# Forty-seven one-pass products appended after the last tile of a two-block transformer kernel

## The reference, cut to what matters

```
merged = jnp.sum(gates * br, axis=2)
x = x + jnp.einsum('bsd,de->bse', merged, w_out[l])
```

## Time and profile before

| | us |
|---|---|
| median of 3 runs | 974.19 |
| lowest and highest run | 973.27, 974.43 |
| span of the profiled execution, first to last instruction | 970.7 |
| median less that span | 3.5 |
| TensorE busy in the span | 960.0 |
| TensorE weight loads busy | 858.6 |
| VectorE busy | 610.2 |
| ScalarE busy | 485.9 |
| GpSimd busy | 216.9 |

### The profile page before, as it was taken

One profiled execution on the slowest core, in us unless ns is written; L12 is line 12 of the kernel. 1 busy time (PEld: TensorE's weight loads), 2 busy tenths in 40 slices (PEclk: granted clock), 3 DMA queues, 4 the chain that ended last, 5 costly groups with the idle time before them and its releaser, 6 DMA issues.

```text
span 970.7 us, 17117 instructions
## 1 busy us (share of the span) xinstructions
PE 960.0 (99%) x7053; PEld 858.6 (88%) x7053; DVE 610.2 (63%) x827; ACT 485.9 (50%) x729; POOL 216.9 (22%) x177
## 2 busy tenths in 40 slices
PE   9999999999999998999999999999999999999998
PEld 8989999999889896899999997778787878999996
DVE  5867554554589899764445447747574646856664
ACT  6446434434364475743443446456545555647452
POOL 0005980000023330000000000414662704920100
PEclk9999999999999999999999999999999999999999
DMA  8764855656554522365565573555455635562461
GB/s 274 221 224 149 275 176 180 196 186 195 190 180 159 175 88 75 126 231 176 186 202 174 186 239 116 198 172 175 142 172 172 190 108 174 176 210 94 136 213 43
DMA packets 119635, 168.73 MB, mean 174 GB/s; under 512 B 5556, under 2 KB 88596, under 8 KB 119572
## 3 DMA queue, kind: packets, MB, share of 16 engines
q1 hardware_dynamic: 119140, 167.66, 53.3%
q10 hardware_dynamic: 432, 0.19, 0.1%
HBM read 165.38 MB, written 2.46 MB: 173 GB/s over the span
## 4 chain that ended last, share of the span: by engine, by line
PE 92%; DVE 4%; ACT 1%; POOL 1%; DMA 1%; issue 1%; SPq 0%; ACTq 0%; DVEq 0%
PE ps L465 26%; PE ps L467 25%; PE ps L466 25%; PE ps L919 2%; PE ps L906 2%; PE ps L892 2%; DVE wlo_sb L445 1%; POOL b_inv_sb L2455 1%; PE ps L553 1%; DMA raw_sb<-w_in_even 1%; PE ps L492 1%; PE ps L566 1%; PE ps L726 1%; PE ps L2077 1%; PE ps L563 1%; PE ps L558 1%
## 5 line engine op out<-in xcount | busy, mean ns | idle before, releaser
L445 DVE TENSOR_TENSOR wlo_sb<-raw_sb,whi_sb 128x2048 fp32r<-128x2048 f32 x143 | 332.7, 2328 | 201.1 <-ACT whi_sb L422 201.1
L422 ACT ACTIVATE whi_sb<-raw_sb 128x2048 fp32r<-128x2048 f32 x143 | 273.9, 1916 | 180.6 <-PE ps L467 163.3
L465 PE MATMUL ps<-hhi_sb,whi_sb 128*128 128x256 f32 x992 | 278.4, 281 | 0.9 <-DVE wlo_sb L445 0.5
L466 PE MATMUL ps<-hlo_sb,whi_sb 128*128 128x256 f32 x992 | 276.9, 279 | 0.0
L467 PE MATMUL ps<-hhi_sb,wlo_sb 128*128 128x256 f32 x992 | 276.8, 279 | 0.0
L465 PEld LDWEIGHTS ps<-hhi_sb,whi_sb 128*128 128x128 f32 x992 | 186.5, 188 | 3.0 <-issue 1.2
L466 PEld LDWEIGHTS ps<-hlo_sb,whi_sb 128*128 128x128 f32 x992 | 186.5, 188 | 0.9
L467 PEld LDWEIGHTS ps<-hhi_sb,wlo_sb 128*128 128x128 f32 x992 | 186.4, 188 | 0.0
L465 PE MATMUL ps<-whi_sb,hhi_sb 128*128 128x512 f32 (+2 forms) x304 | 119.6, 394 | 0.3 <-DVE qkl_sb L2341 0.2
L467 PE MATMUL ps<-whi_sb,hlo_sb 128*128 128x512 f32 (+2 forms) x304 | 116.8, 384 | 0.0
L466 PE MATMUL ps<-wlo_sb,hhi_sb 128*128 128x512 f32 (+2 forms) x304 | 116.7, 384 | 0.0
(11 more groups left out here) (335 smaller groups left out, 1345.8 us busy)
## 6 DMA issues: line engine op xcount, KB each, us to landing
raw_sb<-w_in SPq DMA_DIRECT2D x45, 1024.0 KB, 5.2
raw_sb<-ffn_gate SPq DMA_DIRECT2D x22, 1024.0 KB, 5.3
raw_sb<-ffn_up SPq DMA_DIRECT2D x22, 1024.0 KB, 5.3
raw_sb<-ffn_down SPq DMA_DIRECT2D x22, 1024.0 KB, 5.0
raw_sb<-w_in_even SPq DMA_DIRECT2D x8, 1024.0 KB, 8.4
raw_sb<-w_in_odd SPq DMA_DIRECT2D x8, 1024.0 KB, 5.1
raw_sb<-w_branch SPq DMA_DIRECT2D x6, 1024.0 KB, 5.1
scratch_sb<-bias_rows_dram SPq DMA_DIRECT2D x40, 128.0 KB, 3.0
```

The source lines that it names most:

```text
L422: nc.scalar.activation(place(whi, n0), in_raw(n0), ACT.Copy).then_inc(hi_ready, 1)
L445: nc.vector.tensor_tensor(place(wlo, n0), in_raw(n0), place(whi, n0).bitcast(F32), ALU.subtract).then_inc(lo_ready, 1)
L465: nc.tensor.matmul(dst, l_hi, r_hi, start=first, stop=False)
L466: nc.tensor.matmul(dst, l_hi, r_lo, start=False, stop=False)
```

## The change

Behind the four tiles of the last projection TensorE makes 47 more one-pass products. They read the last weight tile, `w = place(whi, N_OUT2 + 3)`, and 128 columns of `hhi`, both of which are complete by then, and write PSUM bank 6 (in the last eight banks 6 and 7 in turn), which nobody reads afterwards. In front of them stand three waits on the last uses of banks 5 to 7.

```diff
+            w = place(whi, N_OUT2 + 3)
+            s = hhi[:, 6, 0:P]
+            pe.wait_ge(*RELEASED[-1])
+            pe.wait_ge(*RELEASED[-2])
+            pe.wait_ge(*RELEASED[-3])
+            columns = (
+                w[:, 0:256], w[:, 8:264], w[:, 2:258],
+                w[:, 0:512].rearrange("p (a b) -> p a b", b=2)[:, :, 0],
+                w[:, 0:256].rearrange("p (a b) -> p b a", b=2),
+                w[:, 0:256].rearrange("p (a b) -> p b a", a=2),
+                w[:, 0:512].rearrange("p (a b) -> p a b", b=16)[:, ::2, :],
+                w[:, 0:512].rearrange("p (a b) -> p a b", b=8)[:, ::2, :],
+                w[:, 0:256].rearrange("p (a b c) -> p b a c", a=2, c=8),
+                w[:, 0:2048].rearrange("p (a b) -> p b a", a=16)[:, 0:16, :],
+                bc(w[:, 0:16], 16, 1))
+            for v in columns:
+                for _ in range(3):
+                    nc.tensor.matmul(ps[:, 6, 0:256], s, v, start=True, stop=True)
+            for v, l, d in ((w[0:64, 0:256], hhi[0:64, 6, 0:P], ps[:, 6, 0:256]),
+                            (w[:, 0:256], hhi[:, 6, 0:32], ps[0:32, 6, 0:256])):
+                for _ in range(3):
+                    nc.tensor.matmul(d, l, v, start=True, stop=True)
+            for k in range(4):
+                nc.tensor.matmul(ps[:, 6 + k % 2, 0:256], s, w[:, 0:256], start=True, stop=True)
+            for k in range(4):
+                nc.tensor.matmul(ps[:, 6 + k % 2, 0:512], s, w[:, k * 512:k * 512 + 512], start=True, stop=True)
```

## The result

| | before | changed |
|---|---|---|
| median of 4 runs, us | 974.31 | 977.79 |
| span of the profiled execution, us | 970.7 | 976.0 |
| time of that execution, us | not recorded | 977.82 |

The ratio is 1.0041 with a 95% interval from 1.0029 to 1.0053: slower by more than the 0.2% that the prediction set as its line, as forecast, and inside the range. The single number, 978.7, was 0.9 us too high, though the span came out 0.8 us longer than predicted (976.0 against 975.2). These two don't fit together by themselves; experiments 1 and 4 take them up.

A forecast was written before the change was run, and what follows sets the result against it. TensorE, busy 960.0 of 970.7 us, was taken as the bound, with 2.9 us of cover at the end. Appended 5.02 + 0.93 + 0.27 + 1.19 = 7.41 us lengthen the span by 4.52: 974.19 + 4.52 = 978.7 us, range 977.2 to 981.0.

The forecast's parts named there:

- The cover of 2.9 us: Between TensorE's last product and SyncE's drain, appended TensorE work costs nothing for 2.9 us; every us beyond lengthens the span.
- The three waits and the start: Before the added products: waits already met, 0 us (other bound 0.15); first added product starts 0.233 us behind the last one.
- Contiguous products: Added products start 0.117 us apart at 256 columns (43, 5.02 us) and 0.233 at 512 (four, 0.93 us).
- Steps: Twelve added products whose moving operand has a step: 0.216 us each instead of 0.117, 1.19 us more in all.
- the pair: TensorE's moving operand is read two elements at a time; non-adjacent ones are read as two, 0.10 us more a product.
- signs of being wrong: In the profile after: forms 4 and 5 differing from 6 and 10, or any stepped product above 0.25 us, among others.
- The second rival: Only far steps (forms 6 and 10) fall to 0.216 us, forms 4 and 5 don't: +3.9 us, 978.1; chance 0.22.
- Shape changes: Among the added products, three changes of shape, back to full included, cost 0.09 us each, 0.27 us in all.
- Overlap: Added products run two at a time and the cover swallows them: 974.3 to 976.0 us, not slower; chance 0.04.
- The clock: TensorE goes on without a pause at the end, so all 47 added products run at the 2.4 GHz level.
- The sum: 7.41 us of TensorE behind 967.54, plus 0.26 for drain and barrier: span 975.21 against 970.69, 4.52 us more.
- The base: The 3.5 us outside the span stay, so the 4.52 us are added to the median of before, 974.19 us.

The follow-up runs named there:

- experiments 1 and 4: 1: the kernel before run again without edit, 973.40 us against 973.65. 4: the changed kernel run again with more runs, 978.62 us against 973.40 for before.
- Experiment 6: Changed kernel with its 47 products replaced by thirteen moving-operand views, four times each behind four contiguous products; one run, 0.11 to 0.285 us a product.

## Why the prediction was right, point by point

- **The place.** "The cover of 2.9 us" hides what is appended, and what exceeds it is paid in full: shown by 24, 35 and 51 products (0.1, 1.1 and 3.4 us), and by the same 47 costing 7.4 us where there is no cover.
- **The three waits and the start** cost nothing: the first added product starts 0.24 us behind the last real one.
- **Contiguous products** at 0.117 and 0.233 us: as measured, forms 1 to 3, 7 to 9, 11, 14 and 15.
- **Steps.** The step of the argument that failed is the pair: "a pair that isn't adjacent must be read as two". The total survived by luck, because errors of both signs cancel. Twelve products at 0.10 us extra made 1.19 us. Measured: forms 4 and 5 have 6 x (0.231 - 0.117) = 0.68 (forecast 0.59), form 6 nothing (0.30), form 10 3 x (0.27 - 0.117) = 0.46 (0.30): 1.14 us together. Experiment 6 puts four columns a line in the place of the pair, and a surcharge at distances of 256 and 512 bytes for form 10. Two of the prediction's own signs of being wrong came true with that: forms 4 and 5 differ from 6 and 10, and form 10 takes more than 0.25 us.
- **The second rival** (only far steps cost) fails on form 4, which costs 0.23, and on form 6, which costs nothing. Its page, the Trainium skill's "SBUF — State Buffer", section "Specifications (TRN2)", is borne out in that lines are 16 bytes: runs of 4 cost 0.12 us from a boundary and 0.23 from 4 or 8 bytes behind it. Its two hits a line are not enough for TensorE's one-pass products; step 2 has two and costs 0.23. The measurement decides.
- **Shape changes.** The term "3 x 0.09 = 0.27" measured 0.10 + 0.11 into 64 rows and 0.09 + 0.02 on to 128 rows with 32 columns, 0.32 us in all, and nothing for the third: a size slightly off and a rule that was wrong. The earlier trace rows could not tell rows from columns.
- **Overlap** (the case on the other side) didn't happen: no two added products start less than 0.11 us apart. They are 0.117 us apart at 256 columns and 0.23 at 512. The trace disagrees with the 131 ns at 512 columns of the Trainium skill's "TensorE: Matmul & The Clock Gate", section "Back-to-back issue gap", after the change as before.
- **The clock.** The forecast took the 2.4 GHz level for all 47: the granted clock is 1.00 over 967.5 to 976 us.
- **The sum.** 7.41 us of TensorE were forecast; from 968.08 to the last product's start (975.74 less its 0.39) and one more distance of 0.23 are 7.50. The span grew by 4.52 in the forecast and by 4.6 in the trace, and the time by 4.6 at full clock.
- **The base.** "The 3.5 us outside the span stay" was wrong: in all but one of the executions of before that list both it is 1.75 to 1.93 us. Taking 1.8 us for the profiled execution too, the other 1.7 us were the distance from its short span to the median of others; its own time isn't on record. It didn't touch the forecast difference. That 978.7 lies 0.9 us above the measured 977.79 comes from its base: 974.19, the median of before, is 1.1 us above the 973.13 that before has at full clock, and three of the four executions of the changed kernel are at full clock.

## What to carry to other kernels

Work appended to an engine cost nothing here as long as that engine ended before the last store had landed, and what lay beyond was paid in full; find that moment by putting the engine's drain beside the queue that waits for the output. For one-pass fp32 products lay the moving operand out so that each 16-byte line gives four columns close together: 256 columns then took 0.12 us. Views that gave fewer took 0.22 to 0.235 us, and steps of 256 or 512 bytes up to 0.285. Compare a profiled span with its own execution's time, not with a median of others, and compare executions that list the same clock.

## What was not expected of the hardware

- Two places read in turn are slightly faster than contiguous columns: 0.11 against 0.117 us.
- Elements needn't be distinct or in order: each 4th element four times over costs 0.12 us, as if it were contiguous.
- Going between 64 and 128 rows costs some 0.19 us each way, spread over two products, but 0.12 us when it goes into 32 stationary columns; going between 128, 64 and 32 stationary columns at 128 rows costs nothing.
- A mean granted clock of 0.998 instead of 1.000 stands for one dip: half the clock for most of 372 to 376 us, in a kernel that is otherwise at 1.00. It costs 1.2 us, and the same kernel has medians of 973.13 us without and 974.40 us with less than 1.000.
- The warm-up products go from 0.21 to 0.11 us apart at another moment in each execution, with a granted clock listed as 1.00 throughout. Of the 1.1 us that this costs at its worst, 0.2 to 0.4 us are left by 12 us.
